# Adaptive-norm modulation moved between engines and stages of a two-layer encoder step; first-layer attention written out without staging copies

## What is computed

```python
cs = jax.nn.silu(c)
for i in range(DEPTH):
    sh1, sc1, gt1, sh2, sc2, gt2 = jnp.split(cs @ w_ada[i] + b_ada[i], 6, axis=-1)
    h = ada_modulate(rms_norm(x, g_mix[i]), sh1, sc1)
    ...
    x = x + gt1[:, None, :] * o
    h = ada_modulate(rms_norm(x, g_ffn[i]), sh2, sc2)
    x = x + gt2[:, None, :] * swiglu(h, w_ffn_in[i], w_ffn_out[i])
shf, scf = jnp.split(cs @ w_ada_final + b_ada_final, 2, axis=-1)
y = ada_modulate(rms_norm(x, g_final), shf, scf)
```

## Time and profile before

| | |
|---|---|
| median of 3 runs | 1726.47 us (1725.47 to 1726.69) |
| the profiled execution | 1720.86 us, span 1719.0 |
| TensorE matmul busy | 1600.5 us, 93% |
| TensorE weight load busy | 1450.6 us, 84% |
| VectorE busy | 536.0 us, 31% |
| ScalarE busy | 524.4 us, 31% |
| GpSimd busy | 589.6 us, 34% |
| chain that ended last | TensorE 80%, VectorE 7%, ScalarE 5%, DMA 4%, issue 3% |

### The profile page before, as it was taken

One profiled execution on the slowest core, in us unless ns is written; L12 is line 12 of the kernel. 1 busy time (PEld: TensorE's weight loads), 2 busy tenths in 40 slices (PEclk: granted clock), 3 DMA queues, 4 the chain that ended last, 5 costly groups with the idle time before them and its releaser, 6 DMA issues.

```text
span 1719.0 us, 30870 instructions
## 1 busy us (share of the span) xinstructions
PE 1600.5 (93%) x11994; PEld 1450.6 (84%) x11994; DVE 536.0 (31%) x1456; ACT 524.4 (31%) x952; POOL 589.6 (34%) x289
## 2 busy tenths in 40 slices
PE   5888878899999999999988999998989999999997
PEld 3767644469999999999977888887889999999996
DVE  2659546641311111111173444444241111111113
ACT  2433124432422212222253333334242221122223
POOL 2224621125333433334422222223433333333451
PEclk9899989999999999999999999999999999999998
DMA  8427966742222322223213433331213232222221
GB/s 283 111 51 238 290 234 226 264 152 86 62 85 75 96 75 84 73 85 95 66 51 106 122 99 108 89 100 51 62 49 92 80 99 85 62 85 85 87 85 55
DMA packets 240940, 188.41 MB, mean 110 GB/s; under 512 B 12504, under 2 KB 228224, under 8 KB 233584
## 3 DMA queue, kind: packets, MB, share of 16 engines
q1 hardware_dynamic: 228720, 181.49, 34.4%
q10 hardware_dynamic: 12160, 6.09, 1.2%
HBM read 175.44 MB, written 8.50 MB: 107 GB/s over the span
## 4 chain that ended last, share of the span: by engine, by line
PE 80%; DVE 7%; ACT 5%; DMA 4%; issue 3%; SPq 1%; DVEq 0%; ACTq 0%
PE lin L547 68%; DMA ada_raw<-in_w_ada 3%; PE O L781 2%; PE S L732 2%; ACT act_hi L1055 1%; PE O L581 1%; PE T L761 1%; ACT pr_a L1173 1%; DVE sc L1648 1%; DVE pT_a L1749 1%; PE T L607 1%; DMA permb<-rawb 1%; DVE pr_a L1717 1%; DVE pr_a L1699 1%; PE lin L837 0%
## 5 line engine op out<-in xcount | busy, mean ns | idle before, releaser
L1404 POOL TENSOR_TENSOR w_lo<-w_raw,w_hi 128x1024 fp32r<-128x1024 f32 (+2 forms) x186 | 467.8, 2515 | 807.0 <-ACT w_hi L1025 807.0
L547 PE MATMUL lin<-act_hi,w_hi 128*128 128x288 f32 (+1 forms) x2464 | 370.8, 303 | 15.4 <-ACT act_hi L1055 12.1
L547 PEld LDWEIGHTS lin<-act_hi,w_hi 128*128 128x128 f32 (+1 forms) x2464 | 345.5, 193 | 30.4 <-issue 23.9
L547 PE MATMUL lin<-act_hi,w_lo 128*128 128x288 f32 (+1 forms) x2464 | 362.9, 297 | 0.1
L547 PE MATMUL lin<-act_lo,w_hi 128*128 128x288 f32 (+1 forms) x2464 | 357.7, 296 | 0.0
L547 PEld LDWEIGHTS lin<-act_hi,w_lo 128*128 128x128 f32 (+1 forms) x2464 | 338.2, 188 | 6.1 <-issue 4.9
L547 PEld LDWEIGHTS lin<-act_lo,w_hi 128*128 128x128 f32 (+1 forms) x2464 | 336.9, 187 | 2.3 <-issue 1.5
L1025 ACT ACTIVATE w_hi<-w_raw 128x1024 fp32r<-128x1024 f32 (+2 forms) x186 | 204.5, 1100 | 177.0 <-PE lin L547 172.0
L1833 DVE TENSOR_TENSOR hf<-sg,lin 128x576 f32<-128x576 f32 x44 | 33.2, 755 | 443.6 <-PE lin L547 443.6
L1824 DVE SCALAR_TENSOR_TENSOR x<-lin,mods,x 128x288 f32 x144 | 51.3, 412 | 325.5 <-PE lin L547 325.5
L1255 ACT ACTIVATE hid_hi<-hf 128x576 f32 (+1 forms) x44 | 30.1, 685 | 241.0 <-DVE hf L1833 241.0
(11 more groups left out here) (248 smaller groups left out, 1308.5 us busy)
## 6 DMA issues: line engine op xcount, KB each, us to landing
ada_raw<-in_w_ada SPq DMA_DIRECT2D x44, 1024.0 KB, 6.0
w_raw<-in_w_ffn_in SPq DMA_DIRECT2D x88, 512.0 KB, 3.8
w_raw<-in_w_ffn_out SPq DMA_DIRECT2D x32, 704.0 KB, 4.3
w_raw<-in_w_in_b SPq DMA_DIRECT2D x32, 512.0 KB, 4.2
w_raw<-in_w_in_a SPq DMA_DIRECT2D x16, 512.0 KB, 4.0
ada_raw<-in_w_ada_final SPq DMA_DIRECT2D x8, 1024.0 KB, 4.9
bk<-cum_dram SPq DMA_DIRECT2D x16, 416.0 KB, 5.7
w_raw<-in_w_out_a SPq DMA_DIRECT2D x8, 512.0 KB, 4.0
```

Source lines behind the costliest of these rows:

```text
L547: last = nc.tensor.matmul(lin[0:m, u % 2, h, 0:HALF], w, (lo if p == 2 else hi)[:, t, tok], start=(p == 0 and t == 0), stop=(p == 2 and t ...
L1404: TT(w_lo[:, u % 2, 0:n], w_raw[:, u % 2, 0:n], w_hi[:, u % 2, 0:n].bitcast(F32), ALU.subtract)\
```

## The change

It has five parts.

1. Block 1 of the modulation is computed between the index scores: a step after score units 0 and 2 of each of the four linear units. Its loads are spread over SyncE's queue there.
2. Block 2 is computed in layer 0's attention, a step at every third unit (n = 1, 4, 7 to 22), transposed at n = 26.
3. Blocks 3 to 6 leave TensorE. During the first FFN VectorE sums them: for each 128 rows, two operations over 2048 columns (one for each conditioning vector) multiply `ada_raw` by that vector's 128 values of cs (one a partition) and add to `acc`. Each of 32 steps has a slot, after a tile or after an output unit of the first half, or after a tile of the second half; slots 9 and 10, the last two tiles of the first half, have two steps each (`ada_slot_steps`). TensorE then sums over partitions with 8 matmuls a block (`ada_collect`, with `pick` as weights). The loads go into SyncE's queue after the slot's weight loads; each waits until the sums of the step two before are done.
4. Layer 0's attention is written out as 32 units; it reads queries, keys and values in place, and the copies to `qS_a`, `kS_a`, `vS_a` are gone. Its first scores are computed ahead of and within the linear unit of the last query pair, whose rotary work moves from VectorE to GpSimd. `S2` and `T2` change places in `lin`.
5. The scaling of the probabilities moves to GpSimd (`norm_a`); VectorE keeps the reciprocal (`recip_a`). GpSimd's splits of finished pairs stand after the scaling of n = 6, 10 and so on.

The core of the diff:

```diff
+def t_att(n):
+
+    return T_A + n + (n > ADA2_AT)
+
+
+def ada_slot_steps(slot):
+
+    if slot < HT:
+        return [slot] if slot < HT - 2 else [HT - 2 + 2 * (slot - HT + 2), HT - 1 + 2 * (slot - HT + 2)]
+    return [slot + 2]
...
             def ada_load(n, src):
 
-                sp.wait_ge(ada_used, n - 1)
+                if n < 3 * KT + 2:
+                    sp.wait_ge(ada_used, n - 1)
+                else:
+                    sp.wait_ge(ada_acc, 2 * (n - 3 * KT - 1))
                 sp.dma_start(ada_raw[:, n % 2, :], src).then_inc(ada_in[n % 2], 16)
...
             qi_load(3)
+            for n in range(KT, KT + 2):
+                ada_load(n, ada_src(1, n - KT))
             w_load(U_K, wa[:, 1024:1024 + P], KT, P)
             rope_swap(U_QI + 1)
             w_load(U_K + 1, wa[:, 1024 + P:1024 + 2 * P], KT, P)
+            for n in range(KT + 2, KT + 4):
+                ada_load(n, ada_src(1, n - KT))
             rope_swap(U_QI + 2)
             w_load(U_V, wa[:, 1280:1280 + P], KT, P)
...
+            def ada_slot_loads(slot):
+                for k in ada_slot_steps(slot):
+                    ada_load(3 * KT + k, ada_src(3 + k // KT, k % KT))
+
+            wi, wo = i["w_ffn_in"][0], i["w_ffn_out"][0]
+            for half in range(2):
+                u0 = U_F0 + half * FFN_N
+                for t in range(HT):
+                    for g in range(2):
+                        c0 = (half * HT + t) * P + g * DFF
+                        w_load(u0 + 2 * t + g, wi[:, c0:c0 + P], KT, P)
+                    ada_slot_loads(half * (HT + KT) + t)
+                for m in range(KT):
+                    w_load(u0 + 2 * HT + m, wo[half * WCOL:(half + 1) * WCOL, m * P:(m + 1) * P], HT, P)
+                    if half == 0:
+                        ada_slot_loads(HT + m)
 
             wb = i["w_in_b"][0]
...
+            def ada_collect(b):
+
+                pe.wait_ge(ada_acc, 2 * KT * (b - 2))
+                pe.wait_ge(ada_row_done, b)
+                if b == 3:
+                    pe.wait_ge(pick_done, 2)
+                for s in range(2):
+                    for j in range(4):
+                        last = nc.tensor.matmul(O[32 * j:32 * j + 32, 0:512], pick[:, s, :],
+                                                acc[:, b % 2, s, 512 * j:512 * j + 512], start=(s == 0), stop=(s == 1))
                 last.then_inc(ada_used, 1)
 
             def ada_transpose(b, t):
...
                     idx_unit(4 * j + c)
+                    if c % 2 == 0:
+                        ada_step(KT + 2 * j + c // 2)
...
+            pe.wait_ge(kdup_done, 2)
+            s_wait(0)
+            sa_unit(0)
+            lin_part(U_Q + PAIRS - 1, 0, KT, P, act_hi, act_lo)
+            pe.wait_ge(lin_free[(U_OA - 2) % 2], free_count(U_OA - 2))
+            sa_unit(1)
+            lin_part(U_Q + PAIRS - 1, 1, KT, P, act_hi, act_lo)
+            lin_part(U_Q + PAIRS - 1, 2, KT, P, act_hi, act_lo)
+            ada_transpose(1, T_ADA1)
             pe.wait_ge(lin_free[(U_OA - 1) % 2], free_count(U_OA - 1))
-            pe.wait_ge(lin_free[(U_OA - 2) % 2], free_count(U_OA - 2))
-            for n in range(2):
-                s_wait(n, 0)
-                sa_unit(n, 0)
-            ada_transpose(2, T_ADA2)
-            with pe.Fori(0, PAIRS // 2 - 1) as it:
-                a_body(it, False)
-            a_body(PAIRS // 2 - 1, True)
+            pe.wait_ge(cache_in, 16 * 7)
+            for n in range(4 * PAIRS):
+                k, pair = n % 4, n // 4
+                more = n + 2 < 4 * PAIRS
+                if more:
+                    s_wait(n + 2)
+                ta_unit(n)
+                if more:
+                    sa_unit(n + 2)
+                if n % 3 == 1 and n < 3 * KT:
+                    ada_step(2 * KT + n // 3, adaO)
...
+            ffn_half(U_F0, ACT_N1, 0, None, lambda: ada_collect(3), after_first)
+            ada_collect(4)
+            ffn_half(U_F0 + FFN_N, None, HT, lambda: ada_transpose(4, T_ADA[4]), lambda: ada_collect(5), after_second)
...
+            def norm_a(n):
+
+                k = n % 4
+                pool.wait_ge(rinv_done, n + 1)
+                for e in range(2):
+                    last = TS(probs(pr_a, k, e), probs(pr_a, k, e), rinv[:, k, e:e + 1], None, ALU.mult)
+                if k == 0:
+                    last = TS(ps_a[:, :], ps_a[:, :], rinv[:, 0, 2:3], None, ALU.mult)
+                last.then_inc(norm_done, 1)
...
+            for n in range(4 * PAIRS):
+                norm_a(n)
+                if n == 1:
+                    rope(U_Q + PAIRS - 1)
+                if n % 4 == 2 and n >= 6:
+                    split_pair(n // 4 - 1)
...
+            for n in range(4 * PAIRS):
+                k = n % 4
+                if n + 1 < 4 * PAIRS:
+                    recip_a(n + 1)
+                ta_evac(n)
+                if n + 2 < 4 * PAIRS:
+                    max_unit((k + 2) % 4, n + 2, 0, 0, pr_a, ps_a, bias_a, bias_as, (S, S2)[n % 2])
+                if n == ADA2_AT:
+                    ada_mods(2, T_ADA2)
+                    multiplier(1, T_ADA2)
...
+            def ada_sums(slot):
+
+                for k in ada_slot_steps(slot):
+                    b, kt, n = 3 + k // KT, k % KT, 3 * KT + k
+                    dve.wait_ge(ada_in[n % 2], 16 * ((n - KT) // 2 + 1))
+                    if kt == 0 and b >= 5:
+                        dve.wait_ge(ada_used, 3 * KT + b - 4)
+                    for e in range(2):
+                        dst, raw = acc[:, b % 2, e, :], ada_raw[:, n % 2, :]
+                        if kt == 0:
+                            V.tensor_scalar(dst, raw, cs_w[:, 0, e:e + 1], None, ALU.mult).then_inc(ada_acc, 1)
+                        else:
+                            dve.wait_ge(ada_acc, 2 * k - 1 + e)
+                            V.scalar_tensor_tensor(dst, raw, cs_w[:, kt, e:e + 1], dst, ALU.mult, ALU.add)\
+                                .then_inc(ada_acc, 1)
...
+            for half in range(2):
+                u0, slot = U_F0 + half * FFN_N, half * (HT + KT)
+                for t in range(HT):
+                    ffn_tile(u0, half * HT, t)
+                    ada_sums(slot + t)
+                    if half == 1 and t == 1:
+                        ada_mods(4, T_ADA[4])
+                for m in range(KT):
+                    residual_tile(u0 + 2 * HT, 40, m)
+                    if half == 0:
+                        ada_sums(slot + HT + m)
+                        if m == 1:
+                            ada_mods(3, T_ADA[3])
+                    elif m < 2:
+                        ada_mods(5 + m, T_ADA[5 + m])
             for nz, bt in ((2, 3), (3, 5), (4, 6)):
                 multiplier(nz, T_ADA[bt])
...
```

359 lines of the change are left out of this document (141 added, 218 removed).

## The result

The changed kernel takes **1746.3 us** (median of 4 runs, 1742.18 to 1747.03) against 1726.28 for the kernel before beside it: a ratio of 1.0112, 95% interval 1.0094 to 1.0129. It is slower by 1.1%; I had forecast 1728 with a range up to 1743. The profiled execution has a span of 1745.2 us against 1719.0.

What follows compares the result with a forecast made beforehand. It took TensorE to bound the first FFN, with looser stretches in and ahead of the attention, where the chain waits for modulation weights. 1720.9 - 19 - 16 + 37 = 1723, with 5.6 on top 1728 us; range 1712 to 1743.

Steps and rivals of the forecast that it cites:

- Part 1: Stretch up to the attention's first transpose: forecast to gain 19 us (15 to 23), from 239.0 to 219.8.
- the latest of the three: Before the first transpose, three clocks: VectorE's mask 208, TensorE's chain 216, GpSimd's ropes and scaling 219.8, the latest.
- rival 1: First FFN: sums and GpSimd's splits don't collide, SyncE waits cost 15 us, nothing lingers; kernel 1716 us; chance 0.30.
- Part 2: Layer 0's attention loop: forecast to fall from 134 to 118 us, a gain of 16 (9 to 22).
- the scaling on GpSimd: Attention loop: scaling 2 x 512 columns on GpSimd taken as 1.3 us, bounds 0.88 and 2.5.
- my sum of latencies: Attention loop: four units a pair of heads at 2.8, 3.6, 3.9 and 4.3 us, sum 14.6.
- my 118: Attention loop: forecast length in us, from eight pairs of heads and one block's transposes.
- Part 3: First FFN: forecast cost 37 us, from 8.7 of TensorE work, 25 of stalls and 3 of slow restarts.
- 2 for hid_lo: First FFN: about 2 us of stall for hid_lo itself and later output units, within the 25.
- A step of 7 us: First FFN: VectorE's sums take turns with GpSimd's splits, so a step ends 7 us after hid_lo, not 4.7.
- Rival 3: Attention loop: GpSimd's scaling costs its two-input rate, delays each transpose; gain 5 instead of 16, kernel 1739; chance 0.11.
- Rival 2: First FFN: VectorE's backlog from tiles 9 and 10 persists in the output stage; +13 us, kernel 1741; chance 0.17.

Runs made afterwards that it cites:

- before_scale_gpsimd: Kernel before, with only the scaling of the first attention's probabilities moved from VectorE to GpSimd; attention loop 131.5 us against 134.0, ratio 0.9982.
- even_slots: Changed kernel with one modulation step per first-FFN slot, two in the first tile's slot; FFN stretch 456.9 us against 467.3, kernel 1733.5 us.
- even_loads_later: Changed kernel, two sums ahead of the first FFN tile, one step per slot, loads issued behind the next tile's weights; FFN stretch 449.6 us, ratio 1.0025.

## Why the prediction was wrong, point by point

**What bounds the kernel.** Right: the FFN's tiles hid the sums as long as nothing queued, and the loose stretch ahead of the attention gave most of what was forecast.

**Part 1**, forecast -19, measured -15.5, the end of its range of 15 to 23 (its own terms give 219.4 and not 219.8). GpSimd's period was 6.7 us as forecast, and it was the latest of the three. Its first exchange landed at 176.3 instead of 174, and the scaling of unit 0 took 2.3 instead of 1.1. The second is the price error of part 2 once more. The mask was 2.3 late, mainly by small VectorE operations beside GpSimd, without effect. That single-input work on VectorE was not slowed by GpSimd, as rival 1 has it, is not so: the copy at 196.76 had already taken 1.27 us, and 0.32 when nothing stood beside it (before_scale_gpsimd, 200.55).

**Part 2**, forecast -16 with ends of 9 and 22, measured +4.5. Here the prediction failed. The term "the scaling on GpSimd" was mis-sized, and its bounds too: the row of a copy (576 elements in 0.66 us) was taken as the nearest, and the upper end, GpSimd's two-input rate, gave 2.5 us where 3.1 were measured. I took the value nearest to the lower end, and I had the dear end delay only 0.6 us a pair, 5 us in all. At about the price of my sum the loop takes 125.1, so this term is 13.4 of 20.5 us. The remaining 7 were in my sum of latencies, 14.6 us a pair, and are not settled term by term. The unit behind ScalarE's late copy, which I gave 4.3 us "as now", is the best candidate: moving the copy brings 10.7 to 15.0 us, where the sum had 0.7 to 1.5 a pair for it, 6 to 12 in all; and the 15.0 came with a higher clock. With the copy moved and one head scaled the loop takes 110.2, below my 118. How much of a pair's other units shrinks with it stays open; the units' lengths change from pair to pair with the clock. The third omission was the **clock**: I wrote that TensorE runs slow after a wait, but only for the FFN's stalls, and not for a loop from which I took 26 us of TensorE's work. It fell from 0.99 to 0.86, and giving most of it back is worth 2.6 to 5.7 us at the full price, after what the added matmuls cost, and nothing measurable at one head. The price, the copy and the clock overlap, since shorter latencies bring the clock back by themselves: 13.4, 15.0 and 5.7 are not to be added.

**Part 3**, forecast +37, measured +32.3. Mechanism and places were right: three gaps, before tile 10's first unit, the first and the second output unit, each ended by a split whose load was issued late. The sizes were 2.4, 7.7 and 5.4 instead of 5, 10.5 and 7.5 (the 7.7 is 9.6 with the collection, which the 10.5 held), together 15.5, and the "2 for hid_lo" made no gap of its own. That is rival 1's number, 15, but it came by luck and not by its mechanism, for ahead of two of the gaps sums and splits did take turns (timeline of after; the first three rows from 559.5 to 563):

```profile
559.07 5.27 POOL L1428 TENSOR_TENSOR w_lo<-w_raw,w_hi 128x1024 fp32r<-128x1024 f32 x2 [9.25 <-ACT w_hi L1053]
559.60 2.48 DVE L1835 TENSOR_TENSOR hid_lo<-hf,hid_hi 128x576 fp32r<-128x576 f32 x1 [2.04 <-ACT hid_hi L1276]
...
562.00 4.48 DVE L1857 SCALAR_TENSOR_TENSOR acc<-ada_raw,cs_w,acc 128x2048 f32<-128x2048 f32 x1
...
582.59 3.29 DVE L1835 TENSOR_TENSOR hid_lo<-hf,hid_hi 128x576 fp32r<-128x576 f32 x1 [8.65 <-ACT hid_hi L1276]
```

Ahead of the second gap hid_lo took 2.48 us instead of 0.76 and the first sum 4.48 instead of 2.34, 3.9 more in all; ahead of the third hid_lo took 3.29, 2.5 more. A step of 7 us, as my working had it, came at tile 9 (6.7) and in most tiles with one step (6.75), but not at the other two places. Tile 8's step opens block 4; its two operations, with one tensor input each, took 4.6 us together beside a split. At tile 10 the split had held up hid_lo and was over when the sums began (4.61). That takes 2.4 us from the first and from the third gap. Over the 56 sums the mean is 3.10 us against 2.3 alone. So the Trainium skill's rule (SBUF — State Buffer, SBUF: two separate sides), by which the later one fully blocks, fits the rows of two-input operations. The runs even_slots and even_loads_later show the queue as what makes the three gaps; the turns lengthened two of them, and they made the gap that even_loads_later has left. The restarts cost 5.6 (two of 5.65 us for 22 matmuls that take 3.1, and smaller ones), not 3; the collections and transposes 9.2, where my terms, 8.7 without block 3's collection, had 10.6 with it. Gaps, restarts and these make 30.3 of the 32.3; norm 1 is 1.0 longer, and the rest is not assigned.

**The rivals.** Rival 3 (GpSimd's price delays each transpose) had the right mechanism, 0.11, and the wrong size: it gave the loop a gain of 5, and it was a loss of 4.5. I argued against it with a row of another operation. Rival 2 did not occur: no gap in the output stage after the second unit. The Trainium skill (GPSIMD Engine Reference, 4.1 Engine selection) calls one-input work roughly line rate; the trace disagrees: 1562 ns for 512 columns with a scalar per partition against VectorE's 0.44 us (half of 0.88), 3.5 times as long, and the measurement decides.

**The sum.** The profiled span went from 1719.0 to 1745.2: -15.5 + 4.5 + 2.0 + 32.3 + 2.9 = +26.2. The last 2.9 and the 2.0 of the output projection, which starts at the slow clock (16 matmuls in 4.21 us, where 2.40 is usual), I had at nothing; in the experiments the rest of the kernel, unchanged, takes 853.5 to 862.8 us, so the 2.9 is not a finding.

## What to carry to other kernels

When work moves to an engine whose price no row shows, compute the sum at the dear end first and ask what slack the chain has: here some 1.5 us a unit of 512 columns were free, and the next 1.5 cost 13.4 us in all. When matmuls that fill gaps were taken out of this loop of latencies, the gaps remained and the clock fell; look for the next latency (here a 0.2 us copy behind two exponentials, worth 11 to 15 us) before taking the filling away. When a loop's latencies are cut, look at the clock again: here it came back without any filling. In a queue that loads weights and something with a wait of its own, put the waiting load where nothing due soon stands behind it.

## What the runs showed of the hardware

- GpSimd's `tensor_scalar` with a scalar per partition, float32 in place: 602 ns for 128 columns, 923 for 256, 1242 for 384, 1562 for 512, about 2.5 ns a column and 0.28 us; its copy of 576 columns takes 0.66 us. One-input operations on GpSimd are not one class.
- TensorE's granted clock in the attention loop was 0.99 with 32 modulation steps in it and 0.86 with 8. With 14 groups of matmuls added it was 1.00 where they stood and 0.92 over the loop, which was 5.7 us shorter. With one head scaled on GpSimd and ScalarE's copy early it was 1.00 from 246 on with nothing added.
- A VectorE copy of 64x320 elements took 2.23 us beside GpSimd's subtraction (after, 208.10), 1.27 beside the end of a rope operation (before, 196.76), and 0.32 when it began with GpSimd idle (before_scale_gpsimd, 200.55); the two slow ones ended 0.2 us after GpSimd's operation. In the other direction a GpSimd split of 128x1024 took 6.00 us beside VectorE's sums (even_loads_later, 433.99) and 2.39 before.
